# Seven-product units for the middle third of a down projection: a case on Trainium2

## The reference

```
up = rmsnorm(x, g_ffn) @ w_up
upc, ffn_buf_new = causal_conv(ffn_buf, up, ffn_conv_w)
u, gt = jnp.split(upc, 2, axis=-1)
x = x + (jax.nn.silu(gt) * u) @ w_down        # 2816 features -> 1024
y = rmsnorm(x, g_final)
```

## Time and profile before

| | |
|---|---|
| median of 3 runs | 1038.92 us (1038.42 to 1039.87) |
| profiled execution | 1040.4 us, span 1038.7 us |
| TensorE busy | 1026.6 us, 7450 matmuls |
| VectorE busy | 790.4 us |
| ScalarE busy | 550.9 us |
| granted TensorE clock, mean | 0.998 |

### The profile page before, as it was taken

The page is one execution under the profiler, slowest core; times in us unless marked ns, Lnnn a source line. Parts: engine busy times, 40 slices in busy tenths (PEclk is TensorE's granted clock), DMA queues, the critical chain, the costliest instruction groups (busy, mean ns, idle before and its releaser), DMA issues.

```text
span 1038.7 us, 19592 instructions
## 1 busy us (share of the span) xinstructions
PE 1026.6 (99%) x7450; PEld 999.1 (96%) x7450; DVE 790.4 (76%) x1407; ACT 550.9 (53%) x1060; POOL 66.7 (6%) x162
## 2 busy tenths in 40 slices
PE   8999999999999999999999999999999999999996
PEld 8999988888999999999999999999999999999996
DVE  6854669997779889878886876788787896448964
ACT  7455444655554466556555555655555645125744
POOL 0100000000000011100110000011010000000023
PEclk9999999999999999999999999999999999999999
DMA  7211201022643212222132132131346965415354
GB/s 270 100 42 46 102 22 42 22 81 93 216 136 115 97 42 103 82 103 103 52 133 83 42 123 82 42 125 61 116 141 216 314 223 180 136 55 151 87 185 150
DMA packets 63293, 117.21 MB, mean 113 GB/s; under 512 B 5312, under 2 KB 46912, under 8 KB 63168
## 3 DMA queue, kind: packets, MB, share of 16 engines
q1 hardware_dynamic: 59376, 109.99, 31.4%
q10 hardware_dynamic: 3824, 5.96, 1.6%
HBM read 91.03 MB, written 25.95 MB: 113 GB/s over the span
## 4 chain that ended last, share of the span: by engine, by line
PE 93%; DMA 2%; DVE 2%; ACT 1%; issue 0%; SPq 0%; DVEq 0%; ACTq 0%
PE psum L2967 40%; PE psum L3044 10%; PE psum L2697 9%; PE psum L2917 9%; PE psum L3019 7%; PE psum L2996 3%; PE psum L2764 2%; PE psum L2766 2%; PE psum L2935 2%; PE psum L2765 2%; PE psum L2848 2%; PE psum L2808 1%; PE psum L2858 1%; DMA x_sb<-in_x 1%; DMA zb<-act_d 1%; PE psum L2731 1%
## 5 line engine op out<-in xcount | busy, mean ns | idle before, releaser
L2967 PE MATMUL psum<-diff,w_hi 128*128 128x258 f32 x588 | 116.5, 283 | 0.0
L2967 PE MATMUL psum<-h_hi,w_lo 128*128 128x258 f32 x336 | 95.2, 283 | 0.0
L2967 PE MATMUL psum<-h_hi,w_hi 128*128 128x258 f32 x336 | 95.0, 283 | 0.0
L2967 PE MATMUL psum<-diff,w_lo 128*128 128x258 f32 x336 | 94.9, 282 | 0.0
L2967 PE MATMUL psum<-h_lo,w_hi 128*128 128x258 f32 x336 | 94.8, 282 | 0.0
L2967 PE MATMUL psum<-h_hi,act_lo 128*128 128x258 f32 x336 | 94.7, 282 | 0.0
L2967 PE MATMUL psum<-h_lo,act_hi 128*128 128x258 f32 x336 | 94.5, 281 | 0.0
L2967 PE MATMUL psum<-h_hi,act_hi 128*128 128x258 f32 x336 | 94.5, 281 | 0.0
L2967 PEld LDWEIGHTS psum<-diff,w_hi 128*128 128x128 f32 x588 | 94.0, 190 | 0.0
L2967 PEld LDWEIGHTS psum<-h_hi,w_hi 128*128 128x128 f32 x336 | 63.8, 190 | 0.0
L2967 PEld LDWEIGHTS psum<-diff,w_lo 128*128 128x128 f32 x336 | 63.6, 189 | 0.0
(11 more groups left out here) (425 smaller groups left out, 3323.2 us busy)
## 6 DMA issues: line engine op xcount, KB each, us to landing
raw<-in_w SPq DMA_DIRECT2D x76, 512.0 KB, 4.1
zb<-act_d SPq DMA_DIRECT2D x31, 344.0 KB, 5.1
att<-in_w SPq DMA_DIRECT2D x15, 512.0 KB, 4.9
act_d<-x_sb SPq DMA_DIRECT2D x7, 1032.0 KB, 5.2
raw<-in_w SPq DMA_DIRECT2D x18, 384.0 KB, 3.6
act_d<-att SPq DMA_DIRECT2D x10, 516.0 KB, 2.8
x_sb<-in_x SPq DMA_DIRECT2D x8, 516.0 KB, 5.0
x_d<-x_sb ACTq DMA_DIRECT2D x12, 344.0 KB, 2.4
```

The costliest lines, as they stand in the source:

```text
L2967: ins = mm(bank[to, q], a, b, start=(fresh and k == p == 0), stop=(k == HALF - 1 and p == 2), skip_group_check=True)
```

## The change

The middle group becomes four merged units 4 to 7. A unit does tiles 0 and 1 by the seven products, and tile 2 by two plain outputs `m0` and `m1` from the same four split blocks of weights, a11, a12, a21 and a22 (`mid_product`), in the order of `MID_ORDER`. All 11 pairs now get their differences. The middle group has 18 x pieces in place of 12 (numbers 18 to 35; the last group's are now 36 to 53). The parts of a unit have eight homes, which rotate (`MID_HOMES`). The order of x pieces, weight splits, sums and reads on ScalarE and VectorE is written anew at both turns: unit 3 to 4 and unit 7 to 8. Unit 8's own order and the sums for unit 9 are also moved. The diff, cut:

```diff
-MIXED = (0, 1, 2, 3, 7, 8, 9, 10)
+MIXED = tuple(range(NG))
+MID_PARTS = S_PARTS + ("a21", )
+MID_ORDER = ("p1", "p5", "p6", "p2", "m0", "p7", "p3", "p4", "m1")
+MID_HOMES = ({"a11": 7, "S1": 0, "S2": 1}, {"a11": 0, "S1": 1, "S2": 7}, {"a11": 1, "S1": 7, "S2": 0}, {"a11": 7, "S1": 0, "S2": 1})
+def part_home(u, part):
+    if u in MID_UNITS:
+        return {"a12": 2, "S3": 3, "S4": 4, "a22": 5, "a21": 6, **MID_HOMES[u - MID_UNITS[0]]}[part]
+    return S_PARTS.index(part)
+MID_X = ("b11", "D1", "D2", "b21") + T_X + ("D3", "b22", "D4")
+LAST_X = ("D1", "D2", "b11", "b21", "D3", "b22", "D4")
+X_ITEMS = x_items(0, T_X) + x_items(0, S_X) + x_items(1, MID_X) + x_items(2, LAST_X) + x_items(2, T_X)
 # SP: wait of a weight load, and x pieces behind each weight load
+                    sp.wait_ge(down_lo, SPLIT_N[(old, o, oc) if old == "T" else ("S", o, ("a21" if o in MID_UNITS else "S1" if o in LAST_S else "a11", "a22")[oc])])
+                more = {("S", 0): (1, 1), ("S", 1): (1, 1), ("S", 2): (2, 2), ("S", 3): (1, 9), ("S", 5): (2, 3),
+                        ("S", 7): (0, 9), ("S", 8): (1, 1), ("S", 9): (1, 1)}.get((kind, u), (0, 0))[c]
 # ScalarE, unit 3
+                    if p == HALF - 1 and not fin:
+                        item = X_N[1, "D2", 0] - 1
+                        for k, part in enumerate(("a11", "S1", "S2", "a12")):
+                            s_hi(u + 1, part)
+                            item_hi(item + 2 * k)
+                            item_hi(item + 2 * k + 1)
+                        s_hi(u + 1, "S3")
+                        s_hi(u + 1, "S4")
+                        for n in range(item + 8, item + 12):
+                            item_hi(n)
+                        continue
 # ScalarE, units 4 to 7
+                    for u in MID_UNITS:
+                        s_hi(u, "a22")
+                        s_hi(u, "a21")
+                        preload(u)
+                        if u == MID_UNITS[0]:
+                            item = X_N[1, "D4", 0] - 1
+                            item_hi(item)
+                            item_hi(item + 1)
+                        if u < MID_UNITS[-1]:
+                            for part in ("a11", "S1", "S2", "a12", "S3", "S4"):
+                                s_hi(u + 1, part)
...
+                        item, u = X_N[2, LAST_X[0], 0] - 1, LAST_S[0]
+                        item_hi(item)
+                        item_hi(item + 1)
+                        s_hi(u, "a11")
+                        item_hi(item + 2)
+                        item_hi(item + 3)
+                        s_hi(u, "S1")
+                        for n in range(4, 8):
+                            item_hi(item + n)
+                        s_hi(u, "S2")
+                        s_hi(u, "a12")
+                        item_hi(item + 8)
+                        item_hi(item + 9)
+                        s_hi(u, "S3")
+                        for n in range(10, 14):
+                            item_hi(item + n)
+                        s_hi(u, "S4")
 # VectorE, unit 3
+                    if p == HALF - 1 and not fin:
+                        item = X_N[1, "D2", 0] - 1
+                        unit_sums(u + 1)
+                        s_lo(u + 1, "a11")
+                        s_read(u, "p5")
+                        item_lo(item)
+                        item_lo(item + 1)
+                        s_read(u, "p6")
+                        s_lo(u + 1, "S1")
+                        item_lo(item + 2)
+                        item_lo(item + 3)
+                        s_read(u, "p2")
+                        s_lo(u + 1, "S2")
+                        s_read(u, "p7")
+                        item_lo(item + 4)
+                        item_lo(item + 5)
+                        s_lo(u + 1, "a12")
+                        s_read(u, "p3")
+                        item_lo(item + 6)
+                        item_lo(item + 7)
+                        s_lo(u + 1, "S3")
+                        s_read(u, "p4")
+                        s_lo(u + 1, "S4")
+                        for n in range(item + 8, item + 12):
+                            item_lo(n)
+                        continue
 # VectorE, unit 7
+                        item = X_N[2, LAST_X[0], 0] - 1
+                        item_lo(item)
+                        s_read(u, "p5")
+                        item_lo(item + 1)
+                        s_read(u, "p6")
+                        s_lo(u + 1, "a11")
+                        s_lo(u + 1, "S1")
+                        item_lo(item + 2)
+                        item_lo(item + 3)
+                        s_read(u, "p2")
+                        item_lo(item + 4)
+                        mid_read(u, 0)
+                        s_read(u, "p7")
+                        for n in range(5, 8):
+                            item_lo(item + n)
+                        s_lo(u + 1, "S2")
+                        s_read(u, "p3")
+                        s_lo(u + 1, "a12")
+                        item_lo(item + 8)
+                        item_lo(item + 9)
+                        s_lo(u + 1, "S3")
+                        s_read(u, "p4")
+                        item_lo(item + 10)
+                        item_lo(item + 11)
+                        mid_read(u, 1)
 # VectorE, unit 8 (u == LAST_S[0], p == 0, fin)
+                    if u == LAST_S[0]:
+                        s_read(u, "p5")
+                        s_lo(u, "S4")
+                        s_read(u, "p6")
+                        item_lo(X_N[2, "D4", 0] - 1)
+                        item_lo(X_N[2, "D4", 1] - 1)
+                        s_lo(u, "a22")
...
                     elif fin:
-                        s_read(u, "p5")
+                        s_read(u, "p2")
+                        s_read(u, "p7")
+                        s_lo(u + 1, "a11")
                         unit_sums(u + 1)
-                        s_read(u, "p6")
-                        s_lo(u + 1, "a11")
                         s_lo(u + 1, "S1")
-                        s_read(u, "p2")
                         s_lo(u + 1, "S2")
-                        s_read(u, "p7")
                         s_lo(u + 1, "a12")
 # TensorE
+            def mid_product(u, i):
+                pe.wait_ge(down_lo, SPLIT_N["S", u, ("a12", "a21")[i]])
...
+                for c in range(2):
+                    part, x = f"a{i + 1}{c + 1}", T_X[c]
+                    for k in range(n):
+                        for q, (a, b) in enumerate(((wh, xh), (wh, xl), (wl, xh))):
+                            ins = mm(down_ps[T_BANKS[u][i]], a, b, ...)
+                ins.then_inc(down_done, 1)
-            for tp in MID_PAIRS:
-                mid_pair(tp)
+            for u in MID_UNITS:
+                for step in MID_ORDER:
+                    if step[0] == "m":
+                        mid_product(u, int(step[1]))
+                    else:
+                        s_product(u, step)
```

More of the change, by code:

```diff
@@ L329 @@
 T_X = ("t2a", "t2b")
-MID_X = (("b11", "b21"), ("b12", "b22"), T_X)
-X_ITEMS = x_items(0, T_X) + x_items(0, S_X) + x_items(1, T_X) + x_items(1, MID_X[0] + MID_X[1]) + x_items(2, S_X) + x_items(2, T_X)
+MID_X = ("b11", "D1", "D2", "b21") + T_X + ("D3", "b22", "D4")
+LAST_X = ("D1", "D2", "b11", "b21", "D3", "b22", "D4")
+X_ITEMS = x_items(0, T_X) + x_items(0, S_X) + x_items(1, MID_X) + x_items(2, LAST_X) + x_items(2, T_X)
 X_N = numbered(X_ITEMS)
+UNIT_SUMS = (("S1", "a21", "a22"), ("S2", "a11", "S1"), ("S3", "a11", "a21"), ("S4", "a12", "S2"))
 EARLY = 3
 STAGES = 5
-SKIP_U = 47
+SKIP_U = 52
 def stage_of(n):
@@ L391, in bank_free @@
     last, free = {}, {}
-    for key in phases(t_reads, lambda u: [("S", u, b) for b in range(3)]):
-        kind, n, i = key[0], key[1], key[-1]
-        b = S_BANKS[n % 2][i] if kind == "S" else mid_banks(n, key[2])[i] if kind == "M" else T_BANKS[n][i]
+    s_banks = lambda u: [("S", u, b) for b in range(3)]
+    for key in phases(lambda tp: [("T", tp, i) for i in range(2)] if tp in END_PAIRS else [],
+                      lambda u: s_banks(u) + [("T", u, i) for i in range(2)], s_banks):
+        kind, n, i = key
+        b = S_BANKS[n % 2][i] if kind == "S" else T_BANKS[n][i]
         free[key] = last.get(b, 0)
@@ L1622, in _ @@
                         t_copy(7)
-                    if p == HALF - 1:
[L1624 to L1640, removed]
+                    if p == HALF - 1 and not fin:
[9 more added lines that the diff above has]
+                        continue
+                    if p == HALF - 1:
+                        mid_square(u - 1, "p4")
+                        for c in range(2):
+                            t_hi(END_PAIRS[0], c)
+                        for q in ("p2", "p7", "p3"):
+                            mid_square(u, q)
                         continue
@@ L2339, in unit_sums @@
                 if u:
-                    dve.wait_ge(down_lo, SPLIT_N["S", FIRST_S[-1] if u == LAST_S[0] else u - 1, "S4"])
```

(6 more changed lines are left out.)

245 lines of the change are left out of this document (101 added, 144 removed).

## The result

The changed kernel takes 1041.54 us (median of 13 runs, 1039.88 to 1043.63) against 1038.92 (1038.42 to 1040.38) for the kernel before, a ratio of 1.0023 [1.0015, 1.0031]: 0.23% slower. A second set of runs gave 1.0019 [1.0009, 1.0029]. The profiled execution took 1041.16 us, span 1039.3.

What follows compares the result with a forecast made beforehand. TensorE, 99% busy, was taken as the bound, its middle group one unbroken piece on the path. Saving 5.67 us and adding waits of 1.5, 2.2 and 2.8 gave +0.8 us: 1039.7 us, range 1034.8 to 1042.5.

Steps and rivals of the forecast that it cites:

- The 36 matmuls: Middle group: four merged units of 99 matmuls replace pairs of 108, saving 5.67 us wholly on the path.
- Turn one: Into unit 4: p6 waits L - 1.3, L being x piece 33's load time, taken as 2.8; 1.5 us (1.0 to 2.3).
- Turn two: Into unit 8: p6 waits L - 1.5, L being piece 49's load time, taken as 3.7; 2.2 us (1.6 to 3.7).
- The estimate by the Trainium skill: Loads at both turns: about 2.0 us plus bytes at 436 GB/s; waits 1.1 and 1.3 us, change 0.4 us faster.
- Unit 9: Last group: sums moved after unit 8's p7 read delay the p6 read that p7 needs; 2.8 us (1.9 to 3.2).
- Unit 10: Last group: units 10 and 11 keep the order of before, counted from their own p7, and wait no further.
- The work that is hidden: Up stage's 5 us of added differences cost zero; 9.1 us of VectorE work fits each 15.6 us middle unit.
- The sum: Whole change: -5.67 + 1.5 + 2.2 + 2.8 = +0.8 us, 1039.7 us without a profile.
- the waits eat the gain: Main forecast and likeliest case: waits of 3.6 to 7.75 us at both turns and unit 9, time the same; chance 0.48.
- the ring at the loaded latency: Rival: weight loads slow the five-stage x loads at both turns; waits 9.2 us, 1042.5 us; chance 0.24.
- the signs that I named: Breaks before p6 of units 4 and 8 and p7 of unit 9; waits name preload about three times, VectorE's read once.
- The covered case: Rival: TensorE waits for next to nothing; 1033.3 us, or 1034.8 with one 1.5 us wait; chance 0.28.

Runs made afterwards that it cites:

- all three moves: Changed kernel with unit 4's and unit 8's negated copies made earlier and unit 9's sums back before unit 8's p6 read; 1035.66 us, ratio 0.9967.
- the run with the weights held back: Changed kernel with SP waiting for ScalarE's copy of x piece 49 before issuing unit 10's first weights; 1041.59 us, ratio 1.0017.

## Why the prediction was right, point by point

**The 36 matmuls.** Right: 5.67 us. The kernel with all three moves gets 3.4 of them with 2.2 us of pauses left.

**Turn one.** The mechanism and the place were right, and the formula L - 1.3 was 0.2 off (L - 1.1); its own terms add up to 877.4 and L - 1.4, which is 0.3 off. I took 2.8 for L, the executions had 2.3 to 2.9, and the pause was 1.3 to 1.8 for a forecast of 1.5.

**Turn two.** L - 1.5 was right to 0.1 (its terms give L - 1.6). I took 3.7, the executions had 3.0 to 4.8; 2.4 and 3.2 us of pause in the two executions of the changed kernel for a forecast of 2.2. The bounds, 1.6 to 3.7, held both. The reason that I gave for 3.7, the weights behind it, is not borne out: without them the load took 3.9. That 3.7 came near was luck in this respect. Nor were the loads of 2.3 and 3.1 us alone, as I had called them: in the kernel before the next went out 0.4 and 0.8 us behind them. The estimate by the Trainium skill (DMA: Bandwidth & Descriptors, Anatomy of one DMA), 2.4 us for 172 KB and 2.8 us for 344 KB, agrees with the loads of piece 33 (2.3 to 2.9) and not with those of piece 49 (3.0 to 4.8). The forecast that I set beside it, the whole change 0.4 us faster, should have read 0.5 by its own terms; 2.4 us slower was measured.

**Unit 9.** Forecast 2.8 before p7; measured 2.88 in two parts, 1.35 before p6 for ScalarE's copy and 1.53 before p7. With the sums moved back it is 0.33. VectorE's order in it, with the two waits for ScalarE, forecast at 0.3 and 0.6 and measured at 0.29 and 0.37, and the read that p7 needs; this answers to the earlier trace rows:
```profile
957.44 0.69 DVE L2340 TENSOR_TENSOR act_lo<-att,act_hi 128x512 fp32r<-128x512 f32 x1 [0.29 <-ACT act_hi L1430]
...
958.92 0.69 DVE L2342 TENSOR_TENSOR act_lo<-att,act_hi 128x512 fp32r<-128x512 f32 x1 [0.37 <-ACT act_hi L1434]
...
964.11 0.51 DVE L2374 TENSOR_TENSOR x_sb<-x_sb,psum 128x344 f32<-128x344 f32 x1
```
```profile
964.76 0.40 PE L3097 MATMUL psum<-hy_hi,act_hi 128*128 128x344 f32 x1 [1.37 <-DVE x_sb L2374]
```

**Unit 10: the step that failed.** "Units 10 and 11 keep the order of before, counted from their own p7, and wait no further" was wrong: p7 of unit 10 waits 0.43 us for the read of p6 in every kernel with the change. Late in unit 9 VectorE stands idle for ScalarE's copy of an x piece; the kernel before has such a wait a unit later, where it costs nothing, and none here:
```profile
967.87 1.66 DVE L2362 TENSOR_TENSOR h_lo<-zb,h_hi 128x688 fp32r<-128x688 f32 x2 [0.42 <-ACT h_hi L1452]
```
From the read of unit 9's p7 to the end of the read of unit 10's p6 VectorE took 11.4 us, where the kernel before took 10.9; this wait is 0.42 of the 0.5. And I had not looked at the lead there. In the kernel before the same read ended at 977.69 and p7 started about 0.4 us later, where unit 9 had a lead of 1.1:
```profile
977.19 0.50 DVE L2365 TENSOR_TENSOR x_sb<-x_sb,psum 128x344 f32<-128x344 f32 x1
```
That this wait is the cause is read from the order and these times, and not tested. Moving the sums of unit 9 did not remove the pause.

**The work that is hidden.** Right that it is hidden: the up stage costs nothing (ratio 0.9996 alone), and units 5 to 7 run unbroken. The 9.1 us of VectorE work in a unit were too few for unit 5, which makes the sums of two units and has VectorE at 12.2 of 16 us.
```profile
892.00:908.00 16.00, 16.00 (x104) 16.00 (x103) 12.24 (x26) 6.11 (x12) 0.00 (x0) 1.00 0.49 160
```

**The sum.** Forecast 6.5 us of pauses and 1039.7 us; measured 7.5 and 1041.5. The missing 1.0 us of pauses is turn one 0.3, turn two 0.2, unit 9 0.1 and unit 10 0.4. The time is off by 1.8, so 0.8 us lies outside the pauses of the profiled execution. The sum has no term for TensorE's clock, which cost 1.5 us after the pause of unit 8 in some executions and can account for part of it; the rest stays open. With 7.5 to 7.75 us the kernel lies on the border that the text set between "the waits eat the gain" (up to 7.75) and "the ring at the loaded latency" (beyond it), and the measured 0.23% is just outside what I called the same, as 1041.5 is outside the likeliest case's own 1036.8 to 1041.0. The rival's time of 1042.5 needed 9.2 us and both turns at loaded latency; only the second turn came near, in one execution of two. Of the signs that I named, the breaks came where they were forecast, with two more, before p6 of unit 9 and p7 of unit 10; the view of waits names the copy twice and not three times, since it gives unit 4 to VectorE's split, and the read twice and not once, for unit 10. The covered case was never close: with fewer than all three moves no kernel is faster than the one before beyond its interval.

## What to carry to other kernels

When a step is moved behind work that depends on a load, write out the whole line from the engine that frees the buffer, over the load and each queue's operations, to the instruction that is due; here that sum was right to 0.2 us before any landing was known, and the landing (2.3 to 4.8 us) was all that was left uncertain. An operation that needs no load (here a copy of 0.44 us) should stand ahead of the ones that do on an in-order queue: moving two such copies and four sums turned 0.2% slower into 0.3% faster. Where an engine has 12.0 of 13.2 us filled, a moved step of 2.5 us (four sums, 951.7 to 954.2 in the changed kernel) comes back whole as pauses of its consumers: 2.88 us with it, 0.33 without. And a pause of TensorE can cost more than its length: after three of six long ones at unit 8 the granted clock was halved, for 1.5 us more.

## What the runs showed of the hardware that I had not expected

A load with nothing behind it can take as long as one with weights behind it, and its end is slow. From 941 to 944 us in the run with the weights held back, one line for each microsecond, with piece 49 (344 KB, issued at 940.32, landed at 944.2; piece 48, issued before it, landed at 941.9):
```profile
DMA packets 60, 0.09 MB, mean 92 GB/s; under 512 B 4, under 2 KB 59, under 8 KB 59
...
DMA packets 206, 0.27 MB, mean 272 GB/s; under 512 B 8, under 2 KB 206, under 8 KB 206
...
DMA packets 26, 0.03 MB, mean 32 GB/s; under 512 B 8, under 2 KB 25, under 8 KB 25
```
Most of the piece's bytes moved within one microsecond, 942 to 943, and the last 0.03 MB took more than another. Why its end is slow is not shown. The kernel waits for the last packet, so a late end goes into its time, and a long pause can bring the halved clock on top. Both are part of the spread: 1039.7 to 1044.8 us for the changed kernel, 1038.3 to 1041.9 for the one before on the same chip.
